# The norm between two layers of an encoder: x of four row tiles added by an accumulating DMA, and their steps spread out

## The reference

```
for l in range(DEPTH):
    h = rms_norm(x, pre_norm_g[l])
    proj = einsum('bsd,de->bse', h, w_in)          # then attention, gates
    y = einsum('bse,ed->bsd', gated, w_out)
    x = x + rms_norm(y, post_norm_g[l])
rms_norm(x, g) = x * rsqrt(mean(x * x) + 1e-6) * g
```

## Time and profile before

| what | us |
|---|---|
| median of 3 runs | 1242.17 (1241.06 to 1242.97) |
| the profiled execution | 1241.25 |
| its span in the profile | 1239.5 |
| PE busy in the span | 1183.3 |
| DVE, ACT, POOL busy | 808.4, 587.1, 423.5 |

### The profile page before, as it was taken

The page is one execution under the profiler, slowest core; times in us unless marked ns, Lnnn a source line. Parts: engine busy times, 40 slices in busy tenths (PEclk is TensorE's granted clock), DMA queues, the critical chain, the costliest instruction groups (busy, mean ns, idle before and its releaser), DMA issues.

```text
span 1239.5 us, 17639 instructions
## 1 busy us (share of the span) xinstructions
PE 1183.3 (95%) x6480; PEld 1012.3 (82%) x6480; DVE 808.4 (65%) x1711; ACT 587.1 (47%) x1291; POOL 423.5 (34%) x559
## 2 busy tenths in 40 slices
PE   6999999999999998898999999999999999999984
PEld 5988888888888887786888888888888888888873
DVE  4574765747657678767544866848658576585666
ACT  5544444434445466654444453444445445344452
POOL 5333214133174365564642122132131331312313
PEclk9999999999999999998999999999999999999987
DMA  6161201020022153153222011020020210201125
GB/s 209 51 207 37 67 18 51 18 57 29 18 86 68 36 152 118 60 171 108 60 68 73 18 40 51 20 79 26 17 73 18 72 35 18 72 18 56 49 37 102
DMA packets 93845, 79.47 MB, mean 64 GB/s; under 512 B 3104, under 2 KB 84000, under 8 KB 93760
## 3 DMA queue, kind: packets, MB, share of 16 engines
q1 hardware_dynamic: 92896, 75.20, 20.0%
q0 software_dynamic: 864, 3.15, 1.6%
HBM read 69.90 MB, written 13.68 MB: 67 GB/s over the span
## 4 chain that ended last, share of the span: by engine, by line
PE 45%; DVE 4%; ACT 2%; issue 1%; POOL 0%; POOLq 0%; DVEq 0%; ACTq 0%
PE dense L1107 23%; PE dense L1115 7%; PE pv_ps L1224 6%; PE turned L1271 4%; PE scores L1304 4%; DVE o_sb L1816 1%; ACT yT_hi L1466 1%; DVE yT_lo L1827 1%; PE turned L1259 1%; ACT v_st L1417 1%; ACT junk L1584 0%; DVE y L1685 0%; DVE pT_lo L1766 0%; DVE v_st L1761 0%; DVE e_sb L1701 0%
## 5 line engine op out<-in xcount | busy, mean ns | idle before, releaser
L1107 PE MATMUL dense<-hT_hi,w_hi 128*128 128x512 f32 x880 | 351.1, 399 | 0.0
L1107 PE MATMUL dense<-hT_lo,w_hi 128*128 128x512 f32 x880 | 345.0, 392 | 0.0
L1107 PE MATMUL dense<-hT_hi,w_lo 128*128 128x512 f32 x880 | 344.7, 392 | 0.0
L958 POOL TENSOR_SCALAR w_hi<-w_f 128x1024 fp32r<-128x1024 f32 x86 | 94.3, 1096 | 664.4 <-PE dense L1107 574.6
L965 POOL TENSOR_TENSOR w_lo<-w_f,w_hi 128x256 fp32r<-128x256 f32 x344 | 254.2, 769 | 7.2
L1401 ACT ACTIVATE e_sb<-e_sb,low 128x256 f32<-128x256 f32 (+7 forms) x256 | 170.3, 665 | 171.4 <-DVE low L1701 169.8
L1434 ACT ACTIVATE pT_hi<-turned 128x640 fp32r<-128x640 f32 (+3 forms) x224 | 117.2, 523 | 174.4 <-PE pv_ps L1224 97.3
L1107 PEld LDWEIGHTS dense<-hT_hi,w_lo 128*128 128x128 f32 x880 | 165.6, 188 | 36.7
L1107 PEld LDWEIGHTS dense<-hT_hi,w_hi 128*128 128x128 f32 x880 | 166.2, 189 | 26.1 <-issue 0.3
L1107 PEld LDWEIGHTS dense<-hT_lo,w_hi 128*128 128x128 f32 x880 | 166.5, 189 | 25.2
L1766 DVE TENSOR_TENSOR pT_lo<-turned,pT_hi 128x640 fp32r<-128x640 f32 (+3 forms) x224 | 133.7, 597 | 43.0 <-ACT pT_hi L1434 42.0
(11 more groups left out here) (188 smaller groups left out, 1799.8 us busy)
## 6 DMA issues: line engine op xcount, KB each, us to landing
w_f<-in_w_in_c SPq DMA_DIRECT2D x37, 512.0 KB, 4.1
w_f<-in_w_in_ab SPq DMA_DIRECT2D x34, 512.0 KB, 4.0
rel_tiles_dram<-rel_rows_dram SPq DMA_DIRECT2D x1, 5120.0 KB, 24.1
bias<-rel_tiles_dram SPq DMA_DIRECT2D x8, 640.0 KB, 5.3
y<-in_x SPq DMA_DIRECT2D x8, 512.0 KB, 7.7
hT_lo_f<-in_x SPq DMA_DIRECT2D x8, 512.0 KB, 7.1
out_x<-y SPq DMA_DIRECT2D x8, 512.0 KB, 3.8
w_f<-in_w_out_c SPq DMA_DIRECT2D x8, 512.0 KB, 3.7
```

The source lines that it names most:

```text
L958: ts(hi, src, 1.0, 1.0, ALU.mult, ALU.mult).then_inc(w_hi_done, 1)
L1107: last = mm(dense[:, x.n % 2, :], lhs[:, d * P:(d + 1) * P], rhs[:, d, x.f * HALF:(x.f + 1) * HALF], start=i == 0, stop=i == 23)
```

## The change

For row tiles 0 to 3 only:

- In step 104 (B[3].start) SP copies x of these rows to the output rows, DRAM to DRAM. The loads of x into x_place at step 112 go.
- `yg` goes, and `x1` becomes one DVE instruction, y = y * r_y * g_post in place, which no longer reads x.
- In step x1 + 1 POOL issues an accumulating DMA of y onto the output rows, where x already is. It stands behind the inverse roots of that step and ahead of its weight splits.
- In step xsq - 2 SP waits for that DMA and loads x1 from the output rows into x_place. ACT's square waits for this load. The store of x1 by SP goes.
- `scaled` reads x1 from x_place and writes h into y; PE transposes out of y.
- The steps move (ysq stays): row 0 x1 119, xsq 120 to 124, scaled 122 to 126, turns 124 and 125 to 127 and 128; row 1 x1 121, xsq 122 to 126, scaled 124 to 128, turns 126 and 127 to 129 and 130; row 2 x1 125 to 123, xsq 126 to 128, scaled 128 to 130, turns 129 and 130 to 133 and 134; row 3 x1 127 to 125, xsq 128 to 130, scaled 130 to 132, turns 133 and 134 to 135 and 136.
- The last six `out` uses of B[4] and B[5] (row tiles 5 to 7) move from steps 135 to 140 to steps 137 to 142; those of row tile 4 stay at 131 and 132.

```diff
-OUT_STEPS = {0: (3, 4, 6, 7, 8, 9, 11, 12), 2: (3, 4, 5, 6, 7, 8, 9, 10), 4: (3, 4, 7, 8, 9, 10, 11, 12)}
+OUT_STEPS = {0: (3, 4, 6, 7, 8, 9, 11, 12), 2: (3, 4, 5, 6, 7, 8, 9, 10), 4: (3, 4, 9, 10, 11, 12, 13, 14)}
...
-NORM = [Row(0, *b_steps(4.5, 4.6, 4.7, 5.0, 5.2, 5.4)), Row(1, *b_steps(4.7, 5.0, 5.1, 5.2, 5.4, 5.6)),
+NORM = [Row(0, *b_steps(4.5, 4.7, 4.7, 5.4, 5.6, 5.7)), Row(1, *b_steps(4.7, 5.1, 5.1, 5.6, 6.0, 6.1)),
...
 (SP)
-            if s in (B[3].start + 8, B[7].start + 4):
+            if s == B[3].start:
+                for r in range(4):
+                    sp.dma_start(out[rows_of(r), :], x[rows_of(r), :]).then_inc(n_x[r], 16)
+            for n in NORM[:4]:
+                if s == n.xsq - 2:
...
+                    if new(n_added[n.r], 16):
+                        sp.wait_ge(n_added[n.r], 16)
+                    sp.dma_start(x_place(n.r), by_tile(out[rows_of(n.r), :])).then_inc(n_x[n.r], 16)
             for n in NORM:
                 if s == n.xsq:
+                    if n.r < 4:
+                        continue
...
 (POOL)
+            for n in NORM[:4]:
+                if s == n.x1 + 1:
+                    if new(n_x[n.r], 16):
+                        pool.wait_ge(n_x[n.r], 16)
+                    if new(n_sum, n.r + 1):
+                        pool.wait_ge(n_sum, n.r + 1)
+                    nc.gpsimd.dma_start(out[rows_of(n.r), :], y[:, n.r, :], accum_op=ALU.add).then_inc(n_added[n.r], 16)
...
 (ACT, at xsq)
-                    if new(n_sum, r + 1):
-                        act.wait_ge(n_sum, r + 1)
+                    if r < 4:
+                        if new(n_x[r], 32):
+                            act.wait_ge(n_x[r], 32)
...
 (DVE, at x1)
+                    if r < 4:
...
+                        stt(out=y[:, r, :], in0=y[:, r, :], scalar=rowstat[:, 2, r:r + 1], in1=g_post[:], op0=ALU.mult,
+                            op1=ALU.mult).then_inc(n_sum, 1)
+                        continue
 (DVE, at scaled)
-                    stt(out=x_place(r), in0=by_tile(y[:, r, :]), scalar=rowstat[:, 5, r:r + 1], in1=by_tile(g_pre[:]),
+                    to, x1 = (by_tile(y[:, r, :]), x_place(r)) if r < 4 else (x_place(r), by_tile(y[:, r, :]))
+                    stt(out=to, in0=x1, scalar=rowstat[:, 5, r:r + 1], in1=by_tile(g_pre[:]),
```

More of the change, by code:

```diff
@@ L729, in program @@
     n_x, n_stored = [sem(f"norm_x{i}") for i in range(ST)], sem("x1_stored")
+    n_added = [sem(f"norm_added{i}") for i in range(4)]
     n_ysq, n_ymean, n_yr, n_ys, n_sum, n_xsq, n_xmean, n_xr, n_scaled, n_hi = (
@@ L895, in _ @@
             if s == C[1].start + 4:
-                if new(n_ys, ST):
-                    sp.wait_ge(n_ys, ST)
+                if new(n_ys, 4):
+                    sp.wait_ge(n_ys, 4)
+                if new(n_sum, ST):
+                    sp.wait_ge(n_sum, ST)
                 sp.dma_start(g_post[:], post_norm_g[1].partition_broadcast(P)).then_inc(s_gpost, 16)
@@ L930, in _ @@
             if s == C[7].start + 7:
-                if new(n_stored, 16 * ST):
-                    sp.wait_ge(n_stored, 16 * ST)
+                if new(n_stored, 16 * 4):
+                    sp.wait_ge(n_stored, 16 * 4)
+                for r in range(4):
+                    if new(n_x[r], 32):
+                        sp.wait_ge(n_x[r], 32)
                 if new(s_filled, len(FILLS)):
@@ L1139, in spare_use @@
                 for d in range(4):
-                    last = nc.tensor.transpose(dense[:, 2, d * P:(d + 1) * P], x_place(x.row)[:, 4 * x.half + d, :], ident[:])
+                    last = nc.tensor.transpose(dense[:, 2, d * P:(d + 1) * P], by_tile(y[:, x.row, :])[:, 4 * x.half + d, :], ident[:])
             last.then_inc(s_spare, 1)
@@ L1568, in _ @@
                 if s == n.xsq:
[L1569 to L1570 removed]
+                    if r < 4:
+                        if new(n_x[r], 32):
+                            act.wait_ge(n_x[r], 32)
+                    else:
+                        if new(n_sum, r + 1):
+                            act.wait_ge(n_sum, r + 1)
                     if new(n_xsq, r):
@@ L1662, in spare_use @@
             elif u is C[0]:
-                if new(n_stored, 16 * ST):
-                    dve.wait_ge(n_stored, 16 * ST)
+                if new(n_stored, 16 * 4):
+                    dve.wait_ge(n_stored, 16 * 4)
+                for r in range(4):
+                    if new(n_x[r], 32):
+                        dve.wait_ge(n_x[r], 32)
                 last = nc.vector.tensor_copy(into, dense[:, 2, :])
@@ L1895, in _ @@
                 r = n.r
-                if s == n.yg:
+                if s == n.yg and r >= 4:
                     if new(n_ysq, r + 1):
```

35 lines of the change are left out of this document (24 added, 11 removed).

## The result

| | kernel before | changed kernel |
|---|---|---|
| median of 4 runs, us | 1241.62 (1239.93 to 1242.97) | 1250.65 (1249.67 to 1251.84) |
| ratio, with its 95% interval | | 1.0075 [1.0058, 1.0092] |
| profiled span, us | 1239.5 | 1250.0 |
| first out use of step 131 (PE) | 511.14 | 515.11 |
| first matmul of the outs behind the layer (PE) | 560.06 | 568.09 |

The forecast was 1245.3 with a range of 1238.5 to 1250.0: the sign was right, the size a third of what came, and the time lies just outside the range. The profiled execution of the changed kernel, 1251.84 us, is the slowest of its four.

What follows compares the result with a forecast made beforehand. It took DVE to bound PE between 482 and 512 us, with 7.0 us of waits, and the new DMA chain to replace them: 2.3 + 0.8 = 3.1 us, a median of 1245.3 us, range 1238.5 to 1250.

Steps and rivals of the forecast that it cites:

- 1.4 us at step 131: First out of step 131 begins at 512.5 in place of 511.14, held back by the DMA chain of row tile 3.
- 0.9 of turns: Two turns that were done before step 131 now come behind it: 0.9 us.
- 0.8 at step 139: Moved outs delay yT_hi of step 137 on ACT, so PE's out of step 139 starts 0.8 us later.
- By itself this ... would take most of the 7.0 us away: Dropping four yg and spreading turns and scaled would remove most of PE's 7.0 us of waits in steps 124 to 131.
- What bounds (rows 2, 3): Profile readings for 482 to 512 us: DVE sets the pace, and PE's 7.0 us of waits are what can be won.
- The DMA chain, steps 1 to 5: Loads, squares, roots, splits and accumulating DMAs in queue order, from row tile 0's load at 481.53 to step 131's out at 512.5.
- upper bound of 9.9: High end for POOL's two splits of steps 124 and 125: 9.9 us, as now, adding 1.3 us to the forecast.
- How it is shared out doesn't matter: PE stands 9.3 us in all before step 131; a wait at step 127 shortens the one at 131.
- 503.2: Time in us at which PE would reach the out of step 131 if it never waited, two turns now coming later.
- DMA copies, SP's waits at nothing: Step 104's four DRAM to DRAM copies and SP's waits at steps 122 to 128 were claimed to cost nothing.
- The rule on the DMA's length: The skill's formula gives 3.2 us for a 512 KB DMA; the forecast kept the measured 5.5 us for an accumulating one.
- The rule on the shared port: Two-input DVE instructions and POOL's SBUF reads lock each other out; accumulating DMA issues may each wait 1.3 us.

Runs made afterwards that it cites:

- E1: Kernel before with its old data path, but the changed kernel's steps for roots, squares, scaled, turns and the outs of B[4] and B[5]: 1.0058 to the kernel before.
- E9: E1 with square, root and scaled of row tile 0 back in their old steps, its turns staying at 127 and 128: 1.0031 to the kernel before.
- E7: Changed kernel with scaled of row tile 3 in step 133 in place of 132: 1.0051 to the kernel before.
- E5: Kernel before with only the outs of B[4] and B[5] moved, to steps 137 to 142 from 135 to 140: 1.0022 to the kernel before.
- E13: Kernel before with yg of row tiles 0 to 3 cut to 8 of 1024 columns: 0.9993 to the kernel before.
- E12: Kernel before with scaled of row tile 1 in step 125 in place of 124, off the q fill: 0.9998 to the kernel before.
- E14: E1 with yg of row tiles 0 to 3 cut to 8 of 1024 columns: 1.0037 to the kernel before.
- E4: Changed kernel with SP's load of x1 ahead of its step's weight loads and POOL's accumulating DMAs ahead of its step's roots: 1.0027 to the kernel before.
- E6: Changed kernel with unread matmuls filling PE's pauses, 9 in step 126 and 22 in step 127: 1.0078 to the kernel before.
- E15: Kernel before with the four w_lo subtractions of the splits of steps 124 and 125 replaced by one-input scalings: 0.9983 to the kernel before.
- E8: E4 with row tile 3 later: x1 in step 127, square and root in 132, scaled in 133: 1.0029 to the kernel before.
- E10: E8 with scaled of row tile 0 in step 125 in place of 126: 1.0032 to the kernel before.
- E2: Changed kernel with only SP's load of x1 moved ahead of the weight loads of its step: 1.0037 to the kernel before.

## Why the prediction was wrong

**The terms of the sum.** Up to the outs it had 1.4 us at step 131, 0.9 of turns and 0.8 at step 139, 3.1 in all; 8.0 came. Step 131 came 4.0 later, 2.6 more than forecast; step 133 cost 1.4 and stood at nothing; the turns and step 139 were right; pv_ps, the outs themselves and small gaps are the rest.

**"By itself this ... would take most of the 7.0 us away": this step failed.** It credited the new steps with a gain, and so the forecast took the DMA chain for the only thing that holds PE. E1 shows that the steps alone, without the chain, cost 0.58%, 7.2 us. The three parts that traces and runs show: scaled of row tile 0 one step ahead of its turn, behind yg and x1 of row tile 3 (3.3 us, E9 against E1); scaled of row tile 3 on the q fill of iteration 132 (1.5 us in the trace, 3.0 in the ratio, E7, in the changed kernel); the outs (2.7 us, E5, in the kernel before). No run takes all three out of E1 together, so that they make up its 7.2 us is not shown. The prediction noted that the `scaled` on the q fill of iteration 124 goes, and did not look for what comes to stand on the next q fill.

**What bounds (rows 2, 3): the reading was right, the conclusion wrong.** DVE was the engine named in every wait, and the 7.0 us were taken as what relief of DVE could win. The 5.1 us of yg weren't in this stretch either: two of the four lie ahead of it (464.18 and 472.71), one on its edge (482.01), and the one inside stood in time in which DVE would have waited for ACT. E13 takes off nearly all of yg and wins at most 2.4 us; E12 moves the largest wait and wins nothing. A wait names who was last, not by how much the next is behind. The one form in which yg seems to count was the new steps (E14, 2.6 us).

**The DMA chain, steps 1 to 5: mechanism right, sizes short.** Load of row tile 0: it landed after 8.2 us for 6.5, and the square ran from 489.43 where 488.0 was forecast. DMA of row tile 2: issued at 491.44 for 490.0. Two splits: from 492.10 to 502.4, 10.3 us for 8.6, past the upper bound of 9.9. One long DVE instruction was allowed for beside them, the scaled of row tile 0; the x1 of row tile 3 (493.62, 1.75 us), which the change moved to step 125, and a gate product of 2.05 us lay there too. DMA of row tile 3 issued at 503.28 for 500.3; out of step 131 at 515.11 for 512.5. The queues' order was said to decide the case, and reversing it (E4) gives back 6.0 us. But the chain's price was reckoned against a kernel that would otherwise be at 503, and that kernel does not exist: with no chain at all the same steps come to 513.83.

**Left out: what else ACT holds back.** ACT's wait for the load was seen as a matter of the square and of hT_hi. Behind it in the queue stood pT_hi and the exponential of step 126, which PE waited for 2.36 us.

**The outs: 0.8 forecast, 0.79 measured at step 139,** by the mechanism given (yT_hi of step 137 ran at 540.78 after 4.27 us of waiting). Forgotten was its second effect, 0.43 us at the end of the layer, and E5's ratio says 2.7 [1.0, 4.3] for the whole edit.

**"How it is shared out doesn't matter".** The 9.3 us of standing forecast ahead of step 131 were measured as 9.5. That the two agree is luck. With 503.2 for a PE that never waits they give 512.7, and the out came at 515.11: PE would not have been there at 503.2 either, since its granted clock fell to half (0.89 over the stretch, where it was 1.00 before). The forecast has no term for that. It doesn't make step 131 late by itself: PE stood 1.57 us for the chain there, a wait that a faster PE would first have made longer. In E6, with the clock kept up to 505.6, step 131 came 1.1 us sooner.

**DMA copies, SP's waits at nothing:** nothing in the trace speaks against it; between 443 and 545 us no split on POOL shows a wait for its weights, before or now.

**The rule on the DMA's length.** By the Trainium skill (DMA: Bandwidth & Descriptors, Anatomy of one DMA) 512 KB come to an estimate of 3.2 us. Here four accumulating ones landed after 5.2 to 6.2 us, so the row was right.

**The rule on the shared port** (the Trainium skill, SBUF — State Buffer, two separate sides). The gate product of step 125 took 2.05 us beside POOL's w_hi (492.10, 1.32 us), where it took 0.83 before and 0.39 in E15 with POOL at rest; the trace agrees with a lock of that size. E15's scaled (488.07), 1.95 us for 1.28 beside an instruction of POOL with one input (487.91, 1.04 us), fits it too. POOL's issues of the accumulating DMAs took 0.87 to 1.04 us in all runs, so none waited the 1.3 us that the prediction held possible.

One reading of the prediction is off without a part in the sum: not all waits of the earlier trace rows are for bank 2; the 1.1 us is for `scaled` itself.

What stays open: from the end of row tile 3's x1 to the turn of step 129 it is 4.5 us in seven kernels, and in between DVE works nearly without a break; which of its instructions waits for PE's fills there was not taken apart. E8 is 1.5 us ahead of E4 in the trace and not in the time. And the new path with steps that cost nothing was not run.

## What to carry to other kernels

A wait tells who is last, not what removing it is worth: before counting on it, cut the suspected work out whole and time that. When work is moved to other steps, walk the queue of every engine at the new places, for what stands ahead of the moved instruction and what stands behind it, and keep some steps between an instruction and the one that needs it if its queue is full: five steps for scaled of row tile 0 won 3.3 us (E9), two in place of one won nothing (E10). A DMA from which a long chain hangs belongs first in its step's queue (E2 to E4). When a forecast counts a pause, count the clock behind it as well.
